# Walking the moving tiles and the outputs of five matmul stages in another order, with padded weight slots

## The chip, the cores and the metric

One core of one Trainium2 chip runs the whole program. The metric is the device time in microseconds (us); lower is better. "Before" is the kernel as it stood, "after" is the kernel with the change.

## What is computed

The reference is two transformer-like blocks over 512 tokens of width 1024, in float32, with a memory of 256 tokens. What matters here is its list of dense products, because nearly all the time is spent in them:

```
first_block:   proj = rms_norm(x) @ w_in          (front)
               mixers: gated delta rule, sparse attention, convolution
               x += concat(mixers) @ w_out
               x += cross attention with the memory (w_q, w_kv, w_o)
               x += square(relu(rms_norm(x) @ mlp_w1)) @ mlp_w2      (up and dn, in two halves)
second_block:  proj = rmsnorm(x) @ w_in_2, gates, convolution, recurrent unit      (mix)
               merged = sig(..) * (y_a @ w_out_a) + sig(..) * (y_b @ w_out_b)      (merge)
               x += merged @ w_o_2                                                 (w_o)
               x += (silu(h @ w_gate) * (h @ w_up)) @ w_down                       (ffn and down)
               rmsnorm(x)
```

## The kernel before, in words

Activations are held transposed: a tile is 128 features (partitions) by T = 512 tokens (2,048 bytes of each partition). Each activation and each weight is split in two float32r parts, a rounded `hi` and the rest `lo`. A product of a 128x128 weight block with a tile is three matmuls in the one helper `products` (L621 to L628, the matmul itself is L627): hi weights with the hi tile, hi weights with the lo tile, lo weights with the hi tile. All three add to one PSUM bank of 512 columns (`acc0` to `acc7`, in the program `k.ps`). Each matmul has its own weight load of 128 columns (512 bytes of each partition).

The weights arrive in panels of up to 8 blocks (PANEL = 1024 columns, 4,096 bytes). SyncE starts a DMA of a panel to one of two `raw` buffers (L522), ScalarE rounds it to `w_hi` (L1384), VectorE subtracts to get `w_lo` (L1981); in the front GpSimd takes part (L553). `w_hi` and `w_lo` have SPLIT = 4 slots each, and the slots lie back to back (`Panels.slot`, L468 to L471). A slot is handed back by the last matmul of a panel (`s_panel_used`).

`tensor_program` sets the order of TensorE's work by hand; the other engines follow by semaphores. `panel` (L630 to L646) runs a panel's blocks over the tiles t of an activation. Where it matters here, the stages come in this order, with the number of matmuls of 512 columns that each has:

- front, w_out, cross attention: 3 x (192 + 64 + 32 + 32) = 960, among many small matmuls;
- up0 and up1: 16 panels x 8 tiles x 3 = 384 each (`h_hi`, `h_lo` move);
- dn0 and dn1: 8 outputs x 16 tiles x 3 = 384 each (`u_hi`, `u_lo` move);
- mix: 8 turns x 58 blocks x 3 = 1,392 (`h`, and two blocks of `ub` a turn);
- merge: 2 x 8 outputs x 8 tiles x 3 = 384 (`ya`, `yb`);
- w_o: 8 x 8 x 3 = 192 (`mg`);
- ffn: 44 panels x 8 x 3 = 1,056 (`h`);
- down: 8 outputs x 22 tiles x 3 = 528 (`f`).

VectorE reads each finished bank (L2384, L2523, L2546, L2628, L2651, L2670) and hands it back (`acc_free`).

`plan_memory` lays the buffers out by hand. The first of them, `raw`, begins at byte 1,152 of a partition; `w_lo` and `w_hi` follow it at distances that are multiples of 4,096 bytes, so every weight block begins 128 bytes past a multiple of 512. The line `top[0] += (192 - top[0]) % 512` puts `h_hi` 192 bytes past a multiple of 512, and all of `h`, `u`, `f`, `y`, `ya`, `yb` and `mg` follow at multiples of 2,048 bytes. So in every product of these the moving tile begins 64 bytes past the weight block, counted modulo 512. `ub_hi` and `ub_lo` lie in the buffer `sq` instead, 70,432 bytes after `raw`: they begin 288 bytes past the weight block, modulo 512.

Of the kernel before, what the change touches and what calls it, by code (L numbers as in the profile page):

```python
# [18 lines left out]
P = 128  # L19
# [6 lines left out]
EPS = 1e-6  # L26
BLK = 8
PANEL = BLK * P
RAW = 2
SPLIT = 4  # L30
LEAD = 10
# [136 lines left out]
def plan_memory(nc, ctx):  # L168
# [286 lines left out]
class Panels(Count):  # L455
# [159 lines left out]
def tensor_program(nc, k):  # L615
# [5 lines left out]
    blk = k.const[:, C_BLK:C_BLK + P]  # L621
    tri = k.const[:, C_TRI:C_TRI + P]

    def products(out, w_at, wn, a_hi, a_lo, first, last):
# [5 lines left out]
    def panel(out, hi, lo, tiles, first=True, last=True, at=0, done=True, w=T, ready=None):  # L630

        slot = pan.slot().start
        if at == 0:

            e.wait_ge(k.s_split_done, RAW + pan.at(1))
        for n, t in enumerate(tiles):
            if ready:
                e.wait_ge(ready[0], ready[1] + t + 1)  # L640
            mm = products(out, slot + (at + n) * P, P, hi[:, t * w:(t + 1) * w], lo[:, t * w:(t + 1) * w],
                          first and n == 0, last and n == len(tiles) - 1)
        if done:
            mm.then_inc(k.s_panel_used, 1)
            pan.step()
        return mm  # L646
# [419 lines left out]
    for j in range(0, KT, 2):  # L1066

        width = 2 if j == 0 else 1
        for j0 in range(j, j + 2, width):
            outs = [acc.take(e, 4 + (j0 + n) % 2) for n in range(width)]  # L1070
            slots = []
            for n in range(width):
                e.wait_ge(k.s_split_done, RAW + pan.at(1))
                slots.append(pan.slot().start)
                pan.step()
            for t in range(KT):
                if t < HEADS:
                    e.wait_ge(k.s_go_lo, t + 1)
                elif t >= 6:
                    e.wait_ge(k.s_mix_lo, t - 5)  # L1080
                else:
                    e.wait_ge(k.s_att_lo, TT)
                for out, slot in zip(outs, slots):
                    mm = products(out[:], slot + t * P, P, til(k.y_hi, t), til(k.y_lo, t), t == 0, t == KT - 1)
# [55 lines left out]
    def wo_part(tiles, heads):  # L1140

        for n in tiles:
            if heads[0] == 0:
                acc.take(e, n)
                if n % 2 == 0:
                    e.wait_ge(k.s_split_done, RAW + pan.at(1))
                    wo_slots.append(pan.slot().start)
                    pan.step()
            for h in heads:
                e.wait_ge(k.s_ao_lo_done, h + 1)  # L1150
                mm = products(k.ps[n][:], wo_slots[n // 2] + (HEADS * (n % 2) + h) * P, P, til(k.ao_hi, h), til(k.ao_lo, h),
                              h == 0, h == HEADS - 1)
            if h == HEADS - 1:
                mm.then_inc((k.s_wo_first, k.s_panel_used)[n % 2], 1)

# [47 lines left out]
    for a, b in ((0, 4), (4, 6), (6, 7), (7, KT)):  # L1203

        for n in range(2):
            if a == 0:
                acc.take(e, n)
                e.wait_ge(k.s_split_done, RAW + pan.at(1))
                up_slots.append(pan.slot().start)
                pan.step()  # L1210
            for t in range(a, b):
                e.wait_ge(k.s_fed_lo, 3 * KT + t + 1)
                mm = products(k.ps[n][:], up_slots[n] + t * P, P, til(k.h_hi, t), til(k.h_lo, t), t == 0, t == KT - 1)
            if b == KT:
                mm.then_inc(k.s_panel_used, 1)
                if n == 0:
                    sum_squares(4 * KT, 3, k.sqacc)
    for j in range(2, 4):
        panel(acc.take(e, j)[:], k.h_hi, k.h_lo, range(KT))
    for half in range(2):  # L1220

        with e.Fori(0, MTH // 4 - (half == 0)) as i:
            pan.enter(i, 4)
            acc.enter(i, [2, 2, 0, 0, 0, 0, 0, 0])
            for j in range(4):
                panel(acc.take(e, j % 2)[:], k.h_hi, k.h_lo, range(KT))
            pan.leave(MTH // 4 - (half == 0))
            acc.leave(MTH // 4 - (half == 0))
        with e.Fori(0, KT // 2) as i:
            pan.enter(i, 4)  # L1230
            acc.enter(i, [1, 1, 0, 0, 0, 0, 0, 0])
            for j in range(2):
                out = acc.take(e, j)[:]
                ready = (k.s_up_lo, MTH * half)
                panel(out, k.u_hi, k.u_lo, range(0, 8), last=False, ready=ready)
                panel(out, k.u_hi, k.u_lo, range(8, 16), first=False, ready=ready)
            pan.leave(KT // 2)
            acc.leave(KT // 2)

# [6 lines left out]
    def mix_tile(u_lo, opening):  # L1246

        for a, b in zip(MIX_CUTS, MIX_CUTS[1:]):
            e.wait_ge(k.s_split_done, RAW + pan.at(1))
            slot = pan.slot().start  # L1250
            order = list(range(a, b))
            if opening and a < KT <= b:

                order = [n for n in order if n != KT - 1] + [KT - 1]
            for n in order:
                bank, hi, lo, t, first, last = blocks[n]
                if hi is k.ub_hi:
# [4 lines left out]
                mm = products(out[:], slot + (n - a) * P, P, til(hi, t), til(lo, t), first, last)  # L1262
# [16 lines left out]
    for n, (hi, lo) in enumerate(both):  # L1279
        out = acc.take(e, n)  # L1280
        e.wait_ge(k.s_split_done, RAW + pan.at(1))
        slots.append(pan.slot().start)
        for t in range(KT - 1):
            e.wait_ge(k.s_s2_free, t + 1)
            products(out[:], slots[n] + t * P, P, til(hi, t), til(lo, t), t == 0, False)
        pan.step()
    e.wait_ge(k.s_s2_free, KT)
    for n, (hi, lo) in enumerate(both):
        t = KT - 1
        products(k.ps[n][:], slots[n] + t * P, P, til(hi, t), til(lo, t), False, True).then_inc(k.s_panel_used, 1)  # L1290
    for n, (hi, lo) in enumerate(both):
        panel(acc.take(e, 2 + n)[:], hi, lo, range(KT))
    with e.Fori(0, KT // 2 - 1) as i:
        pan.enter(i, 4)
        acc.enter(i, [1, 1, 1, 1, 0, 0, 0, 0])
        for j in range(2):
            for n, (hi, lo) in enumerate(both):
                panel(acc.take(e, 2 * j + n)[:], hi, lo, range(KT))
        pan.leave(KT // 2 - 1)
        acc.leave(KT // 2 - 1)  # L1300


    with e.Fori(0, 2) as i:
        pan.enter(i, 4)
        acc.enter(i, [2, 2, 0, 0, 0, 0, 0, 0])
        for j in range(4):
            panel(acc.take(e, j % 2)[:], k.mg_hi, k.mg_lo, range(KT), ready=(k.s_mg_lo, 0))
        pan.leave(2)
        acc.leave(2)


    for j in range(4):
        panel(acc.take(e, j)[:], k.h_hi, k.h_lo, range(KT), ready=(k.s_fed_lo, 5 * KT))
        if j == 0:
            sum_squares(6 * KT, 5, k.sqacc)
    with e.Fori(0, FFN // 2 - 1) as i:
        pan.enter(i, 4)
        acc.enter(i, [1, 1, 1, 1, 0, 0, 0, 0])
        for j in range(4):
            panel(acc.take(e, j)[:], k.h_hi, k.h_lo, range(KT))  # L1320
        pan.leave(FFN // 2 - 1)
        acc.leave(FFN // 2 - 1)
    with e.Fori(0, KT // 2) as i:
        pan.enter(i, 8)
        acc.enter(i, [1, 1, 0, 0, 0, 0, 0, 0])
        for j in range(2):
            out = acc.take(e, j)[:]
            for a, b in zip(DOWN_CUTS, DOWN_CUTS[1:]):
                panel(out, k.f_hi, k.f_lo, range(a, b), first=a == 0, last=b == FFN,
                      ready=(k.s_f_lo_done, 0))  # L1330
        pan.leave(KT // 2)
        acc.leave(KT // 2)

# [1472 lines left out]
```

## Time and profile before

| | us |
|---|---|
| median of 2 runs | 1629.03 (1627.74 to 1630.31) |
| span of the profiled execution | 1626.4 |
| its own time less its span | not listed; the median stands 2.6 above the span |
| mean granted TensorE clock | 0.997 of full speed |
| TensorE busy with matmuls | 1595.6 (98% of the span) |

A busy TensorE is not a TensorE at its peak: a matmul is booked from its first column to its last result, so neighbours overlap in the record (a 512-column matmul is booked with some 390 ns), and the distance from one start to the next is what counts. The program starts with loads and norms, the front lasts to about 445 us, the dense stages fill 445 to 1,614 us, and the last norm and the output end the span.

### The profile page before, as it was taken

The numbers are of one execution on the slowest core, as the hardware profiler recorded it, in microseconds if no ns is written. First come the engines' busy times: TensorE is split into PE (matmuls) and PEld (weight loads), VectorE is DVE, ScalarE is ACT, GpSimd is POOL, SyncE is SP. The second block draws the span as 40 slices with busy tenths as digits, with TensorE's granted clock in tenths as the row PEclk, the third lists the DMA queues.
The fourth block names the chain that finished last, engine by engine and source line by source line (L and its number), as shares of the span: only waits on it lengthen the run. The fifth ranks groups of instructions, "written<-read, shape, count | busy, mean of one in ns | idle before, by whom it ended". The sixth has DMA issues, their size and how long they took to land.

```text
span 1626.4 us, 21588 instructions
## 1 busy us (share of the span) xinstructions
PE 1595.6 (98%) x7524; PEld 1311.0 (81%) x7524; DVE 912.4 (56%) x1319; ACT 684.1 (42%) x996; POOL 157.1 (10%) x97
## 2 busy tenths in 40 slices
PE   6999999999999999999999999999999999999997
PEld 5888798788788888888888888888888888888886
DVE  4549799765664323444377666666455544444332
ACT  5735554554653213433244545554224434443221
POOL 3445486100000000000000000000000000000000
PEclk9999999999999999999999999999999999999999
DMA  7521100122123232233233333333322323222332
GB/s 286 165 78 65 52 1 2 65 86 96 40 91 103 91 103 90 90 104 103 59 105 106 93 93 93 93 93 104 104 90 91 104 90 102 91 93 86 99 97 77
DMA packets 45665, 149.50 MB, mean 92 GB/s; under 512 B 4784, under 2 KB 5936, under 8 KB 45616
## 3 DMA queue, kind: packets, MB, share of 16 engines
q1 hardware_dynamic: 42240, 139.90, 27.1%
q10 hardware_dynamic: 3376, 8.95, 1.5%
q8 instruction: 31, 0.51, 0.1%
q14 instruction: 18, 0.15, 0.0%
HBM read 146.47 MB, written 2.10 MB: 91 GB/s over the span
## 4 chain that ended last, share of the span: by engine, by line
PE 91%; DVE 6%; DMA 1%; ACT 1%; issue 0%; ACTq 0%; DVEq 0%; SPq 0%
PE acc L627 84%; DVE c_acc L2105 1%; DVE tok L2243 1%; DMA x<-xT 1%; DVE d_score_a L2246 1%; PE acc L938 1%; DVE d_score_b L2246 1%; PE acc L963 1%; PE acc L1113 0%; PE acc L1134 0%; DVE g_x L2229 0%; PE acc L800 0%; PE acc L702 0%; DVE w_lo L1973 0%; DVE x L2681 0%
## 5 line engine op out<-in xcount | busy, mean ns | idle before, releaser
L627 PE MATMUL acc<-h_hi,w_hi 128*128 128x512 f32 x1248 | 492.3, 394 | 1.4 <-issue 0.8
L627 PE MATMUL acc<-h_hi,w_lo 128*128 128x512 f32 x1248 | 491.6, 394 | 0.0
L627 PE MATMUL acc<-h_lo,w_hi 128*128 128x512 f32 x1248 | 488.7, 392 | 0.0
L1981 DVE TENSOR_TENSOR w_lo<-raw,w_hi 128x1024 fp32r<-128x1024 f32 (+2 forms) x241 | 281.5, 1171 | 81.7 <-ACT w_hi L1384 59.7
L1384 ACT ACTIVATE w_hi<-raw 128x1024 fp32r<-128x1024 f32 (+2 forms) x241 | 241.9, 1007 | 178.2 <-PE acc L627 86.4
L627 PEld LDWEIGHTS acc<-h_hi,w_hi 128*128 128x128 f32 x1248 | 234.8, 188 | 54.3 <-issue 3.8
L627 PEld LDWEIGHTS acc<-h_lo,w_hi 128*128 128x128 f32 x1248 | 234.9, 188 | 53.4 <-issue 1.0
L627 PEld LDWEIGHTS acc<-h_hi,w_lo 128*128 128x128 f32 x1248 | 234.9, 188 | 49.2
L627 PE MATMUL acc<-u_hi,w_hi 128*128 128x512 f32 x256 | 100.9, 394 | 0.0
L627 PE MATMUL acc<-u_hi,w_lo 128*128 128x512 f32 x256 | 100.4, 392 | 0.0
L2384 DVE TENSOR_TENSOR x<-x,acc 128x512 f32 x32 | 22.0, 688 | 139.2 <-PE acc L627 138.7
L627 PE MATMUL acc<-u_lo,w_hi 128*128 128x512 f32 x256 | 99.3, 388 | 0.0
L2651 DVE TENSOR_TENSOR f_t<-acc,rstd 128x512 f32<-128x512 f32 x44 | 30.4, 691 | 98.5 <-PE acc L627 98.3
L627 PE MATMUL acc<-f_hi,w_lo 128*128 128x512 f32 x176 | 69.3, 394 | 0.0
L627 PE MATMUL acc<-f_lo,w_hi 128*128 128x512 f32 x176 | 69.0, 392 | 0.0
L553 POOL TENSOR_TENSOR w_lo<-raw,w_hi 128x1024 fp32r<-128x1024 f32 x25 | 61.3, 2452 | 78.5 <-ACT w_hi L1377 78.2
L627 PE MATMUL acc<-f_hi,w_hi 128*128 128x512 f32 x176 | 68.3, 388 | 0.0
L1911 ACT ACTIVATE f_hi<-f_t 128x512 f32 x22 | 13.9, 632 | 116.5 <-DVE f_t L2657 116.5
L1825 ACT ACTIVATE u_t<-u_t 128x512 f32<-128x512 f32 x32 | 20.2, 632 | 93.9 <-DVEq L2526 88.8
L2523 DVE SCALAR_TENSOR_TENSOR u_t<-acc,rstd 128x512 f32<-128x512 f32 x28 | 19.4, 691 | 69.1 <-PE acc L627 69.1
L627 PEld LDWEIGHTS acc<-u_hi,w_lo 128*128 128x128 f32 x256 | 48.1, 188 | 11.3
L627 PEld LDWEIGHTS acc<-u_lo,w_hi 128*128 128x128 f32 x256 | 48.1, 188 | 10.8
(394 smaller groups left out, 2323.1 us busy)
## 6 DMA issues: line engine op xcount, KB each, us to landing
raw<-panels_a SPq DMA_DIRECT2D x112, 512.0 KB, 3.3
raw<-panels_b SPq DMA_DIRECT2D x68, 512.0 KB, 3.3
raw<-mix SPq DMA_DIRECT2D x48, 448.0 KB, 3.4
raw<-mix SPq DMA_DIRECT2D x16, 512.0 KB, 3.7
raw<-down SPq DMA_DIRECT2D x16, 384.0 KB, 3.2
raw<-down SPq DMA_DIRECT2D x16, 320.0 KB, 2.9
x<-xT ACTq DMA_DIRECT2D x4, 1024.0 KB, 9.5
x_rows<-xN ACTq DMA_DIRECT2D x2, 1024.0 KB, 8.6
```

The costliest lines, as they stand in the source:

```text
L553: TTn(lo, raw, hi.bitcast(F32), ALU.subtract).then_inc(k.s_split_done, 1)
L627: mm = e.matmul(out, w[:, w_at:w_at + wn], a, start=first and n == 0, stop=last and n == 2)
L938: e.matmul(k.ps[4 + u % 2][:, 0:(qt + 1) * P], k.d_q[r, (h // 2) * T + qt * P:(h // 2) * T + (qt + 1) * P], k.d_k[r, 0:(qt + 1) * P], star ...
L963: mm = e.matmul(k.ps[(7, 3)[qt % 2]][:, h * 64:(h + 1) * 64], k.d_pt[:, (u % 2) * T + t * P:(u % 2) * T + (t + 1) * P], k.d_v[:, t * 64:(t ...
L1384: A(k.w_hi[:, ahead.slot(w)], k.raw[:, ahead.unsplit(w)], ACT.Copy).then_inc(k.s_weights_hi, 1)
L1825: A(k.u_t[:, (2 + j % 2) * T:(3 + j % 2) * T], k.u_t[:, (j % 2) * T:(j % 2 + 1) * T], ACT.Square).then_inc(k.s_up_sq, 1)
L1981: TTn(lo, raw, k.w_hi[:, ahead.slot(w)].bitcast(F32), ALU.subtract).then_inc(k.s_split_done, 1)
L2105: ins = STT(out=out, in0=y, scalar=w, in1=out, op0=ALU.mult, op1=ALU.add)
L2246: replaced[qt] = link(e.match_replace(scores[qt], tok(TOK_M8 + 8 * qt - 8, 8), scores[qt], TAKEN))
L2384: TTn(x, x, k.ps[b][:], ALU.add).then_inc(k.acc_free[b], 1)
L2523: STT(out=til(k.u_t, j % 2), in0=k.ps[j % 2][:], scalar=0.0, in1=k.rstd[:], op0=ALU.max, op1=ALU.mult).then_inc(k.acc_free[j % 2], 1)
L2651: TTn(til(k.f_t, j + 2 * n), k.ps[b][:], k.rstd[:], ALU.mult).then_inc(k.acc_free[b], 1)
```

## The change

Nothing is computed otherwise: the same three matmuls per block, with the same operands. What is new is the order in which a matmul goes over the 512 columns of its moving tile, with the same order over its output, and the place of the weight slots.

- `walked(ap, (side, run, back))` views 512 columns as `side` parts, each cut into pieces of `run` columns. It goes over the pieces of all parts side by side: piece c of part 0, piece c of part 1, and so on, then piece c + 1; with `back` it begins with the last c. Inside a piece it goes forward. With side 2 the two parts lie 1,024 bytes apart; with side 4 they lie 512 bytes apart. A piece of 4, 8, 16 or 32 columns is 16, 32, 64 or 128 bytes.
- The table ORDER has one entry for each stage: none for front, mix and w_o; (2, 16, back) for up0; (2, 4, back) for dn0; (2, 16, forward) for up1; (1, 16, back) for dn1; (2, 32, back) for merge; (4, 16, back) for ffn; (2, 8, back) for down.
- A slot of `w_hi` and `w_lo` is 64 bytes longer than a panel. `w_hi` begins 256 bytes later, all that follows it 512 bytes later (so `h` stays at 192 modulo 512).

```diff
+SLOT = PANEL + 16
+ORDER = {"front": None, "up0": (2, 16, True), "dn0": (2, 4, True), "up1": (2, 16, False), "dn1": (1, 16, True), "mix": None, "merge": (2, 32, True), "w_o": None, "ffn": (4, 16, True), "down": (2, 8, True)}
...
-    k.w_lo, _ = sb("w_lo", SPLIT * PANEL, F32R)
-    k.w_hi, _ = sb("w_hi", SPLIT * PANEL, F32R)
+    k.w_lo, _ = sb("w_lo", SPLIT * SLOT, F32R)
+    k.w_hi, _ = sb("w_hi", SPLIT * SLOT, F32R)
...
-        at = (self.base + self.n) % SPLIT * PANEL
+        at = (self.base + self.n) % SPLIT * SLOT
...
+def walked(ap, order):
+
+    if order is None or ap.shape[-1] != T:
+        return ap
+    side, run, back = order
+    v = ap.rearrange("p (s c r) -> p c s r", s=side, r=run)
+    return v[:, ::-1] if back else v
...
-            mm = e.matmul(out, w[:, w_at:w_at + wn], a, start=first and n == 0, stop=last and n == 2)
+            at = slot + block * P
+            mm = e.matmul(walked(out, order), w[:, at:at + P], walked(a, order), start=first and n == 0, stop=last and n == 2)
```

The rest of the diff hands the stage's entry of ORDER down to `products`; `blocks`, a new parameter of it, is not used.

## Rows read from the trace of the kernel before

**Rows 1.** The page: span, busy time and share of each engine.

```profile
span 1626.4 us, 21588 instructions
...
PE 1595.6 (98%) x7524; PEld 1311.0 (81%) x7524; DVE 912.4 (56%) x1319; ACT 684.1 (42%) x996; POOL 157.1 (10%) x97
...
PEclk9999999999999999999999999999999999999999
```

**Rows 2.** Chain of waits from 430 us to the end, by line.

```profile
by line: PE acc L627 98.3%; DVE x L2681 0.4%; DVE rstd L1964 0.3%; PE acc L654 0.2%; ACT L1920 0.1%; PE acc L1345 0.1%; DVE w_lo L1981 0.1%; ACT rstd L1390 0.1%; DVE x L2670 0.1%; DVEq L2685 0.1%; ACT sq L1368 0.1%; issue 0.0%; PE acc L1134
```

**Rows 3.** Windows by stage: length, busy PE, PEld, DVE, ACT, POOL; clock, DMA.

```profile
534.02:621.68 87.66, 87.66 (x384) 71.93 (x383) 25.67 (x26) 18.14 (x18) 0.00 (x0) 1.00 0.30 96
621.91:709.58 87.67, 87.67 (x385) 71.94 (x384) 41.04 (x47) 34.29 (x46) 0.00 (x0) 1.00 0.29 96
709.80:797.47 87.67, 87.67 (x385) 71.93 (x383) 35.13 (x40) 26.07 (x32) 0.00 (x0) 1.00 0.29 93
797.70:1118.16 320.46, 319.81 (x1395) 261.52 (x1393) 219.62 (x277) 159.49 (x194) 0.00 (x0) 1.00 0.33 94
1118.39:1206.05 87.66, 87.66 (x384) 71.93 (x383) 43.74 (x53) 21.28 (x24) 0.00 (x0) 1.00 0.31 102
1206.28:1249.99 43.71, 43.71 (x192) 35.87 (x191) 25.94 (x33) 16.98 (x23) 0.00 (x0) 1.00 0.29 96
1250.22:1492.57 242.35, 242.35 (x1059) 198.52 (x1057) 116.02 (x133) 100.58 (x112) 0.00 (x0) 1.00 0.28 93
1492.80:1613.65 120.85, 120.85 (x529) 99.16 (x528) 39.15 (x48) 27.10 (x37) 0.00 (x0) 1.00 0.30 84
```

**Rows 4.** Matmuls that read f_hi: count, durations in ns, first and last start.

```profile
L627 PE MATMUL acc<-f_hi,w_hi x176: 388/388/389, 1492.8 to 1613.0; 128*128 128x512 f32 x176
```

**Rows 5.** Timeline of TensorE around the two ub blocks (start, us).

```profile
900.97 0.39 PE L627 MATMUL acc<-h_hi,w_lo 128*128 128x512 f32 x1
901.20 0.40 PE L627 MATMUL acc<-ub_hi,w_hi 128*128 128x512 f32 x1
...
902.60 0.40 PE L627 MATMUL acc<-h_hi,w_hi 128*128 128x512 f32 x1
```

**Rows 6.** Timeline: float32 matmuls of 512 columns, merged.

```profile
165.85 3.17 PE L800 MATMUL acc<-proj,small_w 128*128 128x512 f32 x7
```

**Rows 7.** Timeline: float32 matmuls of 256 columns, merged.

```profile
411.01 1.89 PE L1113 MATMUL acc<-xk,a_q 128*128 128x256 f32 x8
```

**Rows 8.** Groups by form: mean ns of one such matmul.

```profile
L1113 PE MATMUL acc<-xk,a_q 128*128 128x256 f32 x32 | 7.9, 387 | 0.2 <-ACT a_p L1773 0.2
...
L800 PE MATMUL acc<-proj,small_w 128*128 128x512 f32 x16 | 7.0, 592 | 0.0
```

**Rows 9.** Timeline of TensorE, float32r matmuls of 256 columns.

```profile
22.73 0.28 PE L627 MATMUL acc<-m_hi,w_hi 128*128 128x256 f32 x1
...
24.96 0.28 PE L627 MATMUL acc<-m_lo,w_hi 128*128 128x256 f32 x1
```

**Rows 10.** Waits: who waited for whom, us in total, times, longest.

```profile
ACT w_hi L1384 <- PE acc L627: 86.4, 29, 4.3
...
ACT w_hi L1384 <- DMA raw<-panels_a: 50.3, 15, 6.0
```

**Rows 11.** The page: VectorE's and ScalarE's split of a panel; DMA to landing.

```profile
L1981 DVE TENSOR_TENSOR w_lo<-raw,w_hi 128x1024 fp32r<-128x1024 f32 (+2 forms) x241 | 281.5, 1171 | 81.7 <-ACT w_hi L1384 59.7
L1384 ACT ACTIVATE w_hi<-raw 128x1024 fp32r<-128x1024 f32 (+2 forms) x241 | 241.9, 1007 | 178.2 <-PE acc L627 86.4
...
raw<-panels_b SPq DMA_DIRECT2D x68, 512.0 KB, 3.3
```

**Rows 12.** Timeline of the end.

```profile
1613.42 0.39 PE L627 MATMUL acc<-f_hi,w_lo 128*128 128x512 f32 x1
...
1618.38 5.36 DVE L2681 SCALAR_TENSOR_TENSOR x<-x,vec,acc 128x512 f32<-128x512 f32 x8 [1.33 <-PE acc L1345]
```

More of the change, by code:

```diff
@@ L622, in tensor_program, with products, panel @@
     tri = k.const[:, C_TRI:C_TRI + P]
-    def products(out, w_at, wn, a_hi, a_lo, first, last):
+    def products(out, slot, block, a_hi, a_lo, first, last, order, blocks=KT):
         for n, (w, a) in enumerate(((k.w_hi, a_hi), (k.w_hi, a_lo), (k.w_lo, a_hi))):
-            mm = e.matmul(out, w[:, w_at:w_at + wn], a, start=first and n == 0, stop=last and n == 2)
+            at = slot + block * P
+            mm = e.matmul(walked(out, order), w[:, at:at + P], walked(a, order), start=first and n == 0, stop=last and n == 2)
         return mm
-    def panel(out, hi, lo, tiles, first=True, last=True, at=0, done=True, w=T, ready=None):
+    def panel(out, hi, lo, tiles, first=True, last=True, at=0, done=True, w=T, ready=None, order=ORDER["front"], blocks=KT):
         slot = pan.slot().start
@@ L640, in panel @@
                 e.wait_ge(ready[0], ready[1] + t + 1)
-            mm = products(out, slot + (at + n) * P, P, hi[:, t * w:(t + 1) * w], lo[:, t * w:(t + 1) * w],
-                          first and n == 0, last and n == len(tiles) - 1)
+            mm = products(out, slot, at + n, hi[:, t * w:(t + 1) * w], lo[:, t * w:(t + 1) * w],
+                          first and n == 0, last and n == len(tiles) - 1, order, blocks)
         if done:
@@ L1218, in tensor_program @@
     for j in range(2, 4):
-        panel(acc.take(e, j)[:], k.h_hi, k.h_lo, range(KT))
+        panel(acc.take(e, j)[:], k.h_hi, k.h_lo, range(KT), order=ORDER["up0"])
     for half in range(2):
@@ L1225, in tensor_program @@
             for j in range(4):
-                panel(acc.take(e, j % 2)[:], k.h_hi, k.h_lo, range(KT))
+                panel(acc.take(e, j % 2)[:], k.h_hi, k.h_lo, range(KT), order=ORDER[f"up{half}"])
             pan.leave(MTH // 4 - (half == 0))
@@ L1234, in tensor_program @@
                 ready = (k.s_up_lo, MTH * half)
-                panel(out, k.u_hi, k.u_lo, range(0, 8), last=False, ready=ready)
-                panel(out, k.u_hi, k.u_lo, range(8, 16), first=False, ready=ready)
+                panel(out, k.u_hi, k.u_lo, range(0, 8), last=False, ready=ready, order=ORDER[f"dn{half}"])
+                panel(out, k.u_hi, k.u_lo, range(8, 16), first=False, ready=ready, order=ORDER[f"dn{half}"])
             pan.leave(KT // 2)
@@ L1261, in mix_tile @@
                 out = acc.take(e, bank) if first else k.ps[bank]
-                mm = products(out[:], slot + (n - a) * P, P, til(hi, t), til(lo, t), first, last)
+                mm = products(out[:], slot, n - a, til(hi, t), til(lo, t), first, last, ORDER["mix"], b - a)
             mm.then_inc(k.s_panel_used, 1)
@@ L1289, in tensor_program @@
         t = KT - 1
-        products(k.ps[n][:], slots[n] + t * P, P, til(hi, t), til(lo, t), False, True).then_inc(k.s_panel_used, 1)
+        products(k.ps[n][:], slots[n], t, til(hi, t), til(lo, t), False, True, ORDER["merge"]).then_inc(k.s_panel_used, 1)
     for n, (hi, lo) in enumerate(both):
-        panel(acc.take(e, 2 + n)[:], hi, lo, range(KT))
+        panel(acc.take(e, 2 + n)[:], hi, lo, range(KT), order=ORDER["merge"])
     with e.Fori(0, KT // 2 - 1) as i:
@@ L1297, in tensor_program @@
             for n, (hi, lo) in enumerate(both):
-                panel(acc.take(e, 2 * j + n)[:], hi, lo, range(KT))
+                panel(acc.take(e, 2 * j + n)[:], hi, lo, range(KT), order=ORDER["merge"])
         pan.leave(KT // 2 - 1)
@@ L1306, in tensor_program @@
         for j in range(4):
-            panel(acc.take(e, j % 2)[:], k.mg_hi, k.mg_lo, range(KT), ready=(k.s_mg_lo, 0))
+            panel(acc.take(e, j % 2)[:], k.mg_hi, k.mg_lo, range(KT), ready=(k.s_mg_lo, 0), order=ORDER["w_o"])
         pan.leave(2)
@@ L1312, in tensor_program @@
     for j in range(4):
-        panel(acc.take(e, j)[:], k.h_hi, k.h_lo, range(KT), ready=(k.s_fed_lo, 5 * KT))
+        panel(acc.take(e, j)[:], k.h_hi, k.h_lo, range(KT), ready=(k.s_fed_lo, 5 * KT), order=ORDER["ffn"])
         if j == 0:
@@ L1319, in tensor_program @@
         for j in range(4):
-            panel(acc.take(e, j)[:], k.h_hi, k.h_lo, range(KT))
+            panel(acc.take(e, j)[:], k.h_hi, k.h_lo, range(KT), order=ORDER["ffn"])
         pan.leave(FFN // 2 - 1)
@@ L1329, in tensor_program @@
                 panel(out, k.f_hi, k.f_lo, range(a, b), first=a == 0, last=b == FFN,
-                      ready=(k.s_f_lo_done, 0))
+                      ready=(k.s_f_lo_done, 0), order=ORDER["down"], blocks=b - a)
         pan.leave(KT // 2)
```

10 lines of the change are left out of this document (5 added, 5 removed).

## The prediction, made before the run

> **What bounds the kernel now.** I read the page first: TensorE is busy 98% of a span of 1626.4 us and its granted clock is full in all 40 slices [rows 1]. The chain of waits says whether that matters: from 430 us to the end 98.3% of it is L627, the dense matmuls [rows 2]. The windows by stage show the same without gaps, at a granted clock of 1.00, with VectorE between 0.29 and 0.69 of each stage [rows 3]. So the time of the dense part is the number of matmuls times the distance from one start to the next, and nothing else. In down the matmuls that read `f_hi` with `w_hi` begin at 1492.8 and at 1613.0 us, 176 of them, each followed by two others: 120.2 us / (175 x 3) = 228.9 ns [rows 4]. The other stages agree: 87.66 us for 384 matmuls, 120.85 for 528, less the edges [rows 3].
>
> Is 228.9 ns what 512 columns must cost? The trace has three things beside it.
>
> The float32 matmuls, which are not split in hi and lo. Seven of 512 columns take 3.17 us as a block; less the 592 ns booked for the last, six distances are 2.578 us, 429.7 ns each [rows 6, 8]. Eight of 256 columns take 1.89 us; less 387 ns, seven distances of 214.7 ns [rows 7, 8]. Time goes with the columns and is twice what a column at 2.4 GHz takes (0.417 ns), so a pass over 512 columns costs half of 429.7, that is 214.8 ns, weight loads included. The float32r matmul goes over its columns at twice that speed and lies 14.1 ns above such a pass.
>
> The float32r matmuls of 256 columns: from 22.73 to 24.96 us lie 19 distances of 117.4 ns [rows 9], 10.0 ns above half of 214.7. So the excess is neither fixed per instruction nor quite proportional to the columns.
>
> The `ub` blocks: six matmuls from 901.20 to 902.60 us, 233.3 ns each [rows 5], in the middle of `h` matmuls at 228.9. Weights, clock and form are the same. What differs is where the moving tile begins against the weight block: 288 instead of 64 bytes past it, modulo 512. So the distance depends on addresses in SBUF, by 4.4 ns here. My reading, which no row proves: the moving stream and the load of the next 128 columns of weights, which runs beside every matmul (PEld busy 0.82 of each stage [rows 3]), get in each other's way when TensorE reads at full speed, and how often depends on how the two walk over addresses.
>
> The Trainium skill speaks against this reading. Its page "TensorE: Matmul & The Clock Gate", section "Step-by-step: what each phase is for", says that TensorE reads its moving operand and its weights through two independent SBUF ports, so that loading the next weights takes nothing from the running matmul. By that rule the excess would come from something else and the new order would gain nothing; the address dependence of the `ub` blocks doesn't agree with it, and the rule stands behind my first rival.
>
> **The change, part by part.** It adds no instruction, no wait and no transfer: 7,524 matmuls stay 7,524. It touches 384 x 4 (up0, dn0, up1, dn1) + 384 (merge) + 1,056 (ffn) + 528 (down) = 3,504 matmuls by their order, and the other 2,544 of 512 columns (960 in the front part, 1,392 in mix, 192 in w_o) only by the place of the weight slots.
>
> *The order.* The trace of before has no walked matmul, so I bound it from both sides. Best: the whole excess goes, 14.1 ns x 3,504 = 49 us. Worst: the address generator loses a column's time at each jump. The jumps of one matmul are 512 / run: 32 in up0, up1, dn1 and ffn, 128 in dn0, 16 in merge, 64 in down. In all 384 x (32 + 32 + 32 + 128 + 16) + 1,056 x 32 + 528 x 64 = 159,744 jumps; at 0.417 ns, 67 us lost. A milder bad case is that the walked stages go the way of `ub`: 4.4 x 3,504 = 15 us lost. What picks a value between them is the shape of the walk. A weight load passes over 512 bytes while the matmul passes over 2,048; with two parts side by side the moving stream advances through the addresses of one kilobyte at half its speed, with four parts at a quarter, which is the weight load's own pace (512 bytes in the time of a matmul). Two streams that go at like pace can stay clear of each other; two at unlike pace must meet again and again. That argument favours a gain, but it holds only if both go in the same direction and begin clear of each other, and up1 walks forward where up0 walks back, so at least one of these can't be the matching one. I take 8 ns of the 14.1, somewhat over half: 3,504 x 8 = 28 us less. By stage: up and dn 3.1 us each, merge 3.1, ffn 8.4, down 4.2.
>
> *The slots.* The moving tile now begins 64, 0, 448 and 384 bytes past `w_lo` in slots 0 to 3, modulo 512, and 320, 256, 192 and 128 bytes past `w_hi`, in place of 64 everywhere. In the unwalked stages that can cost as much as it costs `ub` (4.4 ns x 2,544 = 11 us) or gain the like. 64 lies among the new values once, and `ub`'s 288 lies between two of them. I take zero, with both ends in the range. For VectorE, ScalarE and the DMA 64 bytes more between slots change no length.
>
> *Does a faster TensorE get its weights?* A panel of 24 matmuls lasts 24 x 228.9 = 5.49 us and would last 5.30. Its supply is 3.3 us from issue to landing, 1.0 us on ScalarE, 1.2 us on VectorE, with two raw buffers [rows 11]. ScalarE waits for TensorE to free a slot (86.4 us, 29 times), more than for the panels' DMA [rows 10]; both mean that weights are ahead. VectorE has more than half of each walked stage's time to itself [rows 3]. So the gain stays. In mix, where VectorE has 219.6 of 320.5 us, nothing gets faster. The tail after the last matmul of down (1613.42 us to the end of the span, 13.0 us) is VectorE, ScalarE and output and stays [rows 12].
>
> The sum: 1626.4 - 28 + 0 = 1598.4 us of span. The median of the runs stands 2.6 us above the profiled span, so 1601 us.
>
> **The rivals.**
>
> *The order has nothing to do with it.* The excess belongs to float32r at full speed, say to each 128-column load, whatever the order. For: it is the same in every stage with tiles at 64, whatever tile or slot is read. Against: `ub`. Time: 1629, with the slots' 11 us either way.
>
> *The walk frees the stream wholly.* All 14.1 ns go, or 10 and more: 1629 - 35 to 49, that is 1580 to 1594; with a gain in the unwalked stages too, down to 1570. For: the float32 matmuls show that 214.8 ns per 512 columns is to be had with loads beside them, and the walked pace can equal the load's. Against: the different entries for like stages, which can't all match.
>
> *Each jump costs.* Place: L627 in dn0 first, which has 128 jumps a matmul, then down and ffn. Price: at one column's time a jump, dn0 20 us (49,152 jumps), down 14, ffn 14, in all 67, so 1696 us without a gain and 1668 with the 28. From 28 us / 159,744 = 0.18 ns a jump the change is slower than before. For: the output jumps as well as the input, and PSUM has not been written so in any row. Against: no row shows a jump costing anything, and pieces of 4 columns or more leave neighbours together. The Trainium skill bears on this one, on its page "Advanced Engine Details and Errata", section "Memory Cachelines": SBUF lines are of 16 bytes and PSUM's of 8, and "Any non-contiguous AP significantly slows down matmuls"; its next line softens this to two consecutive elements being enough. By the first sentence dn0 would be much slower, by the second nothing would; no run here shows either yet.
>
> **How the numbers follow.** The forecast, a gain of 3 to 10 ns on the walked matmuls (1594 to 1619 us with the slots at zero), gets 0.45. Nothing: 0.2. The whole excess: 0.22. Slower: 0.13, of which 0.08 over 2%. What a measurement of this kernel can tell from no change is about 2%, 33 us. Faster by over 2% means under 1596.4: the 0.22 and a third of the forecast's share with help from the slots, 0.38 in all. Slower by over 2% 0.08, the rest, 0.54, within. The range is 1577 to 1636: the whole excess in all walked stages less a little, to no gain with the slots' loss.
>
> **What would show it.** Right: matmuls that read `f_hi` about 221 ns apart and down some 116.6 us long, ffn some 234, dn0 and dn1 each 84.6; mix (320.5) and w_o (43.7) as before; as many instructions. The jump rival shows in dn0 alone first: its window grows from 87.7 to 108. The slots show in mix and w_o, which walk as before: a change there is theirs. If the stages differ among each other by more than 5 ns a matmul, the order's fit and not the walk as such decides. Wrong altogether: a lower granted clock, or stretches in which TensorE waits for `w_lo`.

## The result: slower by 2.7%, and the profile after

The median of the changed kernel is 1673.76 us (1673.48 to 1674.03) against 1629.03 (1627.74 to 1630.31): ratio 1.0274, 95% interval 1.0256 to 1.0292. Slower by 45 us, where I had forecast 28 us less, with a range that ended at 1636. Experiments whose time is given without a ratio were run once; their distances are read from the trace of that run.

The page of the changed kernel, its head:

```profile
span 1671.7 us, 21588 instructions
...
PE 1640.4 (98%) x7524; PEld 1316.4 (79%) x7524; DVE 914.8 (55%) x1319; ACT 684.1 (41%) x996; POOL 157.2 (9%) x97
...
PEclk9999999999999999999999999999999999999999
```

The instructions are as many as before, the granted clock is as high [rows 1], and the chain of waits from 430 us on is the dense matmuls again (the helper's line is L639 now):

```profile
by line: PE acc L639 98.2%; DVE x L2693 0.4%; DVE rstd L1976 0.3%; PE acc L666 0.2%; PE acc L1146 0.1%; ACT L1932 0.1%; PE acc L1357 0.1%; DVE w_lo L1993 0.1%; ACT rstd L1402 0.1%; DVE x L2682 0.1%; DVEq L2697 0.1%; ACT sq L1380 0.1%; issue
```

So no new wait took the time; the matmuls stand further apart. The windows by stage, changed kernel, each from the first matmul of a stage to the first of the next (stretch, length, busy PE, PEld, DVE, ACT, POOL, clock, DMA share, GB/s), in the order up0, dn0, up1, dn1, mix, merge, w_o, ffn, down:

```profile
447.70:537.27 89.57, 89.57 (x388) 72.40 (x386) 50.47 (x58) 40.91 (x55) 0.00 (x0) 1.00 0.29 99
537.27:635.09 97.82, 97.82 (x385) 72.77 (x384) 25.67 (x26) 18.21 (x18) 0.00 (x0) 1.00 0.27 86
635.09:727.25 92.16, 92.16 (x385) 72.81 (x384) 41.06 (x47) 34.29 (x46) 0.00 (x0) 1.00 0.26 91
727.25:817.57 90.32, 90.32 (x385) 72.16 (x384) 35.15 (x40) 26.04 (x32) 0.00 (x0) 1.00 0.28 90
817.57:1140.40 322.83, 322.26 (x1395) 261.93 (x1394) 220.12 (x277) 159.54 (x194) 0.00 (x0) 1.00 0.32 94
1140.40:1231.28 90.88, 90.88 (x385) 72.40 (x384) 43.65 (x53) 21.25 (x24) 0.00 (x0) 1.00 0.29 99
1231.28:1275.54 44.26, 44.26 (x194) 36.10 (x193) 25.95 (x33) 16.96 (x23) 0.00 (x0) 1.00 0.28 95
1275.54:1527.19 251.65, 251.65 (x1060) 200.93 (x1059) 116.07 (x133) 100.45 (x112) 0.00 (x0) 1.00 0.27 89
1527.19:1658.95 131.76, 131.76 (x529) 100.34 (x528) 39.17 (x48) 27.11 (x37) 0.00 (x0) 1.00 0.28 77
```

[Rows 3] end at a stage's last start, one distance of 0.23 us earlier, but for down; counted alike, dn0 grew by 9.9 us, down by 10.9, ffn 9.1, up1 4.3, merge 3.0, dn1 2.4, up0 0.8, and the stages that walk as before grew too: mix 2.1, w_o 0.3. With 2.4 in the front that is the 45.3 us between the spans. Length by count gives the distance from one start to the next: dn0 97.82 us / 384 = 254.7 ns, down 131.76 / 528 = 249.5, against 228.9. The distances below are taken in this way, or as the mean of the distances within a stage where a stage has a wait.

The waits fit weights that were ahead all the time: ScalarE waits for TensorE to free a slot for 150.0 us, 44 times, not for 86.4 [rows 10].

A distance given for a stage is a mean over its matmuls. In the kernel before, the successive distances in dn0 are 232, 226 and 229 ns over and over, with a nanosecond or so between repeats; their mean is the 228.9.

### The profile page after: what moved, and what is told of

Same layout as the page of the kernel before. It is cut to its first block, busy times and chain, and to the rows that moved or that the text cites. A ratio compares the mean times of both kernels' runs of the same rounds, so it can differ in the third digit from the quotient of the medians.

```text
span 1671.7 us, 21588 instructions
## 1 busy us (share of the span) xinstructions
PE 1640.4 (98%) x7524; PEld 1316.4 (79%) x7524; DVE 914.8 (55%) x1319; ACT 684.1 (41%) x996; POOL 157.2 (9%) x97
## 4 chain that ended last, share of the span: by engine, by line
PE 91%; DVE 5%; DMA 2%; ACT 1%; issue 0%; ACTq 0%; DVEq 0%; SPq 0%
PE acc L639 84%; DVE c_acc L2117 1%; DVE tok L2255 1%; DMA x<-xT 1%; DVE d_score_a L2258 1%; PE acc L950 1%; DVE d_score_b L2258 1%; PE acc L975 0%; DMA raw<-panels_a 0%; PE acc L1125 0%; PE acc L1146 0%; DVE g_x L2241 0%; DVE w_lo L1985 0%; PE acc L812 0%; PE acc L714 0%
## 5 line engine op out<-in xcount | busy, mean ns | idle before, releaser
L639 PE MATMUL acc<-h_hi,w_hi 128*128 128x512 f32 x1248 | 499.3, 400 | 1.3 <-issue 0.8
L639 PE MATMUL acc<-h_hi,w_lo 128*128 128x512 f32 x1248 | 495.2, 397 | 0.0
L639 PE MATMUL acc<-h_lo,w_hi 128*128 128x512 f32 x1248 | 495.0, 397 | 0.0
L639 PEld LDWEIGHTS acc<-h_hi,w_hi 128*128 128x128 f32 x1248 | 236.0, 189 | 59.6 <-issue 3.8
L639 PEld LDWEIGHTS acc<-h_hi,w_lo 128*128 128x128 f32 x1248 | 235.8, 189 | 55.9
L639 PEld LDWEIGHTS acc<-h_lo,w_hi 128*128 128x128 f32 x1248 | 235.8, 189 | 55.6 <-issue 1.0
L639 PE MATMUL acc<-u_lo,w_hi 128*128 128x512 f32 x256 | 104.8, 409 | 0.0
L639 PE MATMUL acc<-u_hi,w_lo 128*128 128x512 f32 x256 | 104.6, 408 | 0.0
L639 PE MATMUL acc<-u_hi,w_hi 128*128 128x512 f32 x256 | 104.5, 408 | 0.0
L639 PE MATMUL acc<-f_hi,w_hi 128*128 128x512 f32 x176 | 73.1, 415 | 0.0
L639 PE MATMUL acc<-f_hi,w_lo 128*128 128x512 f32 x176 | 73.0, 415 | 0.0
L639 PE MATMUL acc<-f_lo,w_hi 128*128 128x512 f32 x176 | 72.9, 414 | 0.0
L639 PEld LDWEIGHTS acc<-u_hi,w_lo 128*128 128x128 f32 x256 | 48.5, 189 | 14.4
L639 PEld LDWEIGHTS acc<-u_lo,w_hi 128*128 128x128 f32 x256 | 48.3, 189 | 14.4
```

The source lines that it names most:

```text
L639: mm = e.matmul(walked(out, order), w[:, at:at + P], walked(a, order), start=first and n == 0, stop=last and n == 2)
```

## Experiments

### The two halves of the change

`pad_only` has an ORDER of nothing but None; `walk_only` has the slots back to back:

```diff
-SLOT = PANEL + 16
+SLOT = PANEL
```

> The slots padded, nothing walked. The stages that the change leaves unwalked (mix, w_o) became 1.5 to 1.6 ns a matmul slower in the changed kernel. Theory 'the slots alone do that': every dense stage goes from 228.9 to about 230.4 ns, 6,048 matmuls x 1.5 ns = 9 us, so about 1638 us. Theory 'the walked stages around them do it': 1629 us, and mix stays at 228.9.

Measured: 1639.59 us, ratio 1.0059 (1.0042 to 1.0076). Every dense stage stands at 230.5 to 230.7 ns; mix and w_o:

```profile
802.49:1125.35 322.86, 322.29 (x1396) 261.94 (x1395) 220.09 (x277) 159.55 (x194) 0.00 (x0) 1.00 0.32 94
1213.88:1258.18 44.30, 44.30 (x193) 36.09 (x192) 25.95 (x33) 16.95 (x23) 0.00 (x0) 1.00 0.28 95
```

These are the changed kernel's lengths to 0.04 us. The slots alone cost 9 us. Sorted by slot, the matmuls of dn0 show four mean levels: 229.6, 227.1, 233.2 and 232.3 ns for slots 0 to 3, where before all were 228.9. The moving tile lies 64, 0, 192 and 128 bytes past the weight block there, modulo 256; modulo 512 the blocks of `w_hi` and `w_lo` lie 256 bytes apart. In slot 0 the tile begins 64 bytes past `w_lo` and 320 past `w_hi`, and the three products still have the distances of before, 231.7, 225.7 and 229.3 ns (231.6, 225.7 and 229.3): a shift by 256 bytes changed nothing.

> The order of the change on slots that lie back to back again. Theory 'walk and slots add up': dn0 some 253, down some 248, ffn 236.5, up1 238.5 ns a matmul, mix and w_o back at 228.9; in all 45 - 9 = 36 us over before, 1665. Theory 'the walk clashes with the padded slots, each was fitted to the other's absence': the walked stages come down to 229 or below, 1625 or less. If the pads help the walk (the matmul finds its place against the load), the walked stages get slower than in the changed kernel, over 1674.

Measured: 1672.77 us, ratio 1.026 (1.0243 to 1.0277). Mix is back at 229.1 and w_o at 229.0; the walked stages stand at up0 228.3, dn0 251.1, up1 240.0, dn1 237.8, merge 236.7, ffn 236.0, down 260.0. dn0 and down:

```profile
534.85:631.27 96.42, 96.42 (x386) 73.15 (x384) 25.67 (x26) 18.11 (x18) 0.00 (x0) 1.00 0.27 87
...
1520.34:1657.59 137.25, 137.25 (x529) 100.32 (x528) 39.16 (x48) 27.09 (x37) 0.00 (x0) 1.00 0.26 74
```

Neither theory as I put it: the halves don't add up (43 + 9 is over 45), since the pads bring down from 260.0 to 249.6 and dn1 from 237.8 to 235.2, and cost ffn, dn0 and up0 1.5 to 3.7 ns. The walk is most of the loss.

### Which side pays: the read or the write

```diff
# moving_only
-            mm = e.matmul(walked(out, order), w[:, at:at + P], walked(a, order), ...
+            mm = e.matmul(out, w[:, at:at + P], walked(a, order), ...
# output_only
+            mm = e.matmul(walked(out, order), w[:, at:at + P], a, ...
```

> Padded slots; only the moving tile is walked, the output goes in order, so each product's columns land permuted (the result is another one). Theory 'read side' (moving stream against weight load): the stages keep the distances of the changed kernel, dn0 254.8, down 249.6, up1 240.0, merge 236.7, total about 1674. Theory 'write side' (jumps in PSUM): all fall back to about 230.4 ns, total about 1638.

> Padded slots; only the output is walked, the moving tile goes in order (columns land permuted, the result is another one). Theory 'read side': about 230.4 ns in every stage, about 1638 us. Theory 'write side': dn0 254.8, down 249.6 ns and about 1674 us. If both sides cost, the two halves' excesses add up to that of the changed kernel.

Measured: 1675.65 and 1638.97 us (both leave the columns of a product out of order). dn0 and down, with only the moving tile walked:

```profile
538.44:636.26 97.82, 97.82 (x385) 72.77 (x384) 25.66 (x26) 18.21 (x18) 0.00 (x0) 1.00 0.27 86
1528.40:1660.16 131.76, 131.76 (x529) 100.35 (x528) 39.15 (x48) 27.12 (x37) 0.00 (x0) 1.00 0.27 77
```

and with only the output walked:

```profile
537.19:625.73 88.54, 88.54 (x386) 72.19 (x385) 25.67 (x26) 18.13 (x18) 0.00 (x0) 1.00 0.30 95
1502.72:1624.43 121.71, 121.71 (x530) 99.25 (x529) 39.17 (x48) 27.11 (x37) 0.00 (x0) 1.00 0.30 83
```

The first pair repeats the changed kernel to the hundredth, the second the kernel with the pads alone. All of the walk's price is on the read of the moving tile; jumping in PSUM costs nothing in the seven orders of the change, whose pieces are of 16 bytes and more (dn0 and down above). That disagrees with the Trainium skill's "Any non-contiguous AP significantly slows down matmuls" (page "Advanced Engine Details and Errata", section "Memory Cachelines"). Its next line, by which every two consecutive elements should be contiguous, is not contradicted: all these pieces hold at least four, and no run walked the output alone in shorter ones.

### Does the weight load take part?

`short_loads` loads fewer columns of weights in some stages; in `fixed_plain` and `fixed_walk` every load keeps its 128 columns, but reads the same one:

```diff
# short_loads, with m = 64 (dn0, up1, down) or 32 (dn1)
+                mm = e.matmul(walked(out[0:m], order), w[:, at:at + m], walked(a, order), ...
# fixed_plain, fixed_walk
+            mm = e.matmul(walked(out, order), w[:, at:at + 1].broadcast_to([P, P]) if a.shape[-1] == T else w[:, at:at + P], walked(a, order), ...
```

> Slots back to back. dn0 loads 64 columns of weights a matmul and dn1 32, in the plain order; up1 (walked 2,16 forward), down (2,8 back) load 64; ffn (4,16 back) keeps 128 as control; the output rows of the columns left out aren't computed. The moving reads stay as they were. Theory 'the weight load meets the moving stream': the excess over 214.8 ns falls with the load, dn0 from 14.1 to about 7 (222 ns), dn1 to about 3.5 (218), up1 from 25 to about 12.6 (227), down from 45 to about 23 (237). Theory 'the moving stream alone, it trips over its own jumps': dn0 and dn1 228.9, up1 240.0, down 260.0, ffn 236.0 as in the run with the walk alone.

Measured (1651.63 us; dn0 and dn1 walk plainly here): dn0 228.3, up1 240.0, dn1 231.7, down 245.3, ffn 236.0. Halving the load left the plain order (within 0.6 ns) and up1 where they were, quartering it made dn1 slower, and only down fell, by 14.7 of its 45 ns. The load is not a thing whose length is paid for. (A load of 64 or 32 columns also takes another form of the array, 128x64 and 128x32 in the records, so this run alone would not decide.)

> Slots back to back, plain order; each 128-column weight load of the 512-column products reads one column 128 times over, and so stays in one place of SBUF in place of passing over 512 bytes (all outputs of a product become equal: another result). The moving reads stay. Theory 'where the load reads decides whether it meets the moving stream': the 14.1 ns over the float32 pass change, to about 216 ns if a load that stands still meets it hardly ever. Theory 'a load costs its 128 columns wherever it reads' or 'the moving stream alone': 228.9 ns in every stage.

> The same fixed loads, with the order of the change, slots back to back. Moving stream alone: every stage as with the walk alone, up0 228.3, dn0 251.1, up1 240.0, dn1 237.8, merge 236.7, ffn 236.0, down 260.0. Loads against the stream: all of them move; up1 and merge, which didn't answer to the offset of the slots nor (up1) to a load of half the columns, are the ones that should stay if any do.

Measured (1645.40 and 1663.86 us): plain 231.7 ns in every stage but mix (231.5), where the load that moves on had 228.9; walked, up0 231.0, merge 233.4, dn1 233.3, ffn 235.0, down 240.0, but dn0 251.1 and up1 240.0 as before. dn0, up1 and down of `fixed_walk`:

```profile
537.43:633.85 96.42, 96.42 (x386) 73.15 (x385) 25.67 (x26) 18.12 (x18) 0.00 (x0) 1.00 0.27 87
633.85:726.01 92.16, 92.16 (x385) 72.20 (x384) 41.06 (x47) 34.31 (x46) 0.00 (x0) 1.00 0.27 91
1522.63:1649.34 126.71, 126.71 (x529) 99.79 (x528) 39.16 (x48) 27.09 (x37) 0.00 (x0) 1.00 0.28 80
```

So there are two parts. Where the load reads from matters in most stages (down: 20 ns of its excess, 260.0 to 240.0), and the plain order changed too, though a load itself is booked with 189 ns, against 188 where it reads its 128 columns. That disagrees with the rule of the Trainium skill's page "TensorE: Matmul & The Clock Gate", section "Step-by-step: what each phase is for", that the prediction weighed, by which a load takes nothing from the running matmul. up1 is the other part: 240.0 ns in all six runs that walk it as the change does, with padded slots and without, with half a load, with the load on one column, and at offset 0. There the price is the moving stream's own. dn0 has 251.08 ns with either load too, but it isn't free of the load: with the pads its slots stand at 254.3, 252.6, 256.5 and 255.6 ns.

### A grid of orders

A stage is a cell; each kernel changes the table ORDER alone. All at offset 64 with slots back to back, `grid_d` at offset 0.

> Slots back to back, another order in each stage, as cells of a grid: up0 (1,4,back), dn0 (1,8,back), up1 (1,64,back), dn1 (1,128,back), mix (1,32,back), merge (2,8,forward), w_o (4,16,forward), ffn (2,64,back), down (2,16,back). Known at the same offset: plain 228.9, (1,16,back) 237.8, (2,16,back) 228.3, (2,16,forward) 240.0, (2,32,back) 236.7, (4,16,back) 236.0, (2,8,back) 260.0, (2,4,back) 251.1. Theory 'a jump has a price': the excess falls with the length of the piece, (1,128) near 229 and (1,4) over 245. Theory 'it is the way the two streams meet': no such order by length; down with (2,16,back) must repeat 228.3, else the cells of different stages can't be compared.

> Slots back to back; orders that were seen in one stage are put into another: up0 (2,8,back), 260.0 in down; dn0, w_o and ffn (2,16,back), 228.3 in up0 and 233.3 in down; up1 (2,4,back), 251.1 in dn0; down (1,8,back), 233.3 in dn0; new are dn1 (4,4,back) and merge (4,8,back). If order and offset alone set the distance: the same figures again. If the panels' cut matters (down has 6, 6, 5, 5 blocks a panel, so its tiles and blocks stand otherwise to each other by 512 bytes): up0 differs from 260.0, and dn0, w_o and ffn agree with up0's 228.3. If pieces 1,024 bytes apart are the costly thing and not short pieces: all pairs with 4 or 8 columns stay over 250, down stays at 233, and (4,4) and (4,8) cost as much as the pairs.

> Slots back to back, offset 64; the distance between the parts is varied with short pieces: up0 (8,4,back) 256 bytes apart, dn0 (16,4,back) 128, up1 (8,8,back), dn1 (4,4,forward), merge (32,4,back) 64, w_o (4,64,back), ffn (8,16,back), down (4,4,back). Known: (1,4) 233.3, (2,4) 251.1, (4,4) 271.0, (2,8) 245.3 and 260.0, (4,8) 233.3. Theory 'reads that alternate between places far apart clash': the excess of pieces of 4 falls from (4,4) over (8,4) and (16,4) to (32,4), which with parts of 64 bytes is near to the plain order. Theory 'only the number of jumps counts': all three with pieces of 4 have 128 jumps and cost alike; already against it is (1,4) at 233.3. Direction: (4,4,forward) against 271.0 back.

Measured: 1647.16, 1662.77 and 1711.32 us. Distances in ns, with plain at 228.9; parts of 512 / side columns:

| pieces of | 1 part | 1,024 B apart | 512 B | 256 B | 128 B | 64 B |
|---|---|---|---|---|---|---|
| 16 bytes, back | 233.3 | 251.1 | 271.0 | 277.8 | 240.2 | 220.0 |
| 32 bytes, back | 233.3 | 245.3 / 260.0 | 233.3 | 266.8 | 237.0 | 233.3 |
| 64 bytes, back | 237.8 | 228.3 / 233.3 | 236.0 | 237.8 | 237.9 | |
| 128 bytes, back | 233.4 | 236.7 | | | | |
| 256 bytes, back | 228.9 | 229.0 | 228.9 | | | |

(The cells of 32 bytes at 128 B and 64 B, and of 64 bytes at 128 B, come from `grid_e` below.) Forward: (2,8) 243.3, (2,16) 240.0, (4,16) 236.5, (4,4) 269.3. The worst and the best window of `grid_c`, up0 (8,4,back) and merge (32,4,back):

```profile
445.90:553.52 107.62, 107.62 (x387) 74.46 (x386) 50.77 (x58) 42.75 (x55) 0.00 (x0) 1.00 0.24 82
...
1172.30:1256.79 84.49, 84.49 (x386) 71.92 (x384) 43.75 (x53) 21.26 (x24) 0.00 (x0) 1.00 0.31 106
```

Each of the six orders in the first row has 128 pieces a matmul, and they lie between 220 and 278 ns: a jump has no price of its own. All that differs between these six is how far apart the places are between which the reads alternate. The distance doesn't simply fall with the step, as the first theory of `grid_c` had it: 256 bytes apart is worse than 512. Pieces of 256 bytes cost nothing with up to four parts. Two things did not come out as I expected. (2,16,back) had 228.3 to 228.4 in four stages and 233.3 in down, and (2,8,back) 245.3 in up0 and 260.0 in down: order and offset modulo 512 alone don't set the distance. The cut that `grid_b` suspected (down's panels hold 6, 6, 5 and 5 blocks) is not the reason: in the first panel of each output tile and block go in step as in the other stages, and its matmuls stand at 260.0 and 233.3 ns like the rest of down. What the plan of memory leaves is that `f_lo` lies 45,056 bytes behind `f_hi`, where the other walked tiles have 16,384 or 32,768; no run tests that. (1,8), (2,4) and (4,4), each seen in two stages, did repeat. So most cells are one stage's figure, and a cell may be off by 5 to 15 ns elsewhere. And the distance is not a smooth function of anything in the table.

### The better offset

> Order of the change, slots back to back, activations 128 and not 192 bytes past a multiple of 512, so that moving tiles begin where the weight blocks do (modulo 512). In the run with padded slots alone the slot at this offset had 227.1 ns, the ones at 64, 128 and 192 (modulo 256) 229.5, 232.3 and 233. Theory 'offset and order act together': each stage moves, dn0 by the run with both changes 251 to 253, up0 to about 233, dn1 to about 233.5. Theory 'offset and order are separate': every stage 1.8 ns below the run with the walk alone.

> The kernel before with activations 128 bytes past a multiple of 512: no walk, no pad, moving tile and weight block begin together modulo 512. If the offset sets the distance: 227.1 ns a matmul in every dense stage, 6,048 x 1.8 ns = 11 us less, about 1618 us. If slot 1's 227.1 came from its neighbours in the padded run: no change, 1629 us.

```diff
-    top[0] += (192 - top[0]) % 512
+    top[0] += (128 - top[0]) % 512
```

`plain_at0`: 1618.55 us, ratio 0.9939 (0.9923 to 0.9956); 226.7 to 226.8 ns in every dense stage but mix, whose `ub` blocks keep their place (227.1). In down:

```profile
1480.79:1600.47 119.68, 119.68 (x529) 99.10 (x528) 39.16 (x48) 27.09 (x37) 0.00 (x0) 1.00 0.30 84
```

Nearly all single distances of down are 226 or 227 ns now, where they were 225 to 232. The offset moves the distance in the plain order. `walk_at0`: 1668.14 us; up0 230.4, dn0 253.3, up1 240.0, dn1 233.3, merge 236.7, ffn 239.9, down 251.7. Offset and order act together, up1 and merge excepted, which don't answer to the offset at all.

> Plain order, activations 128 past a multiple of 512, slots padded by 16 bytes: moving tile less weight block is 0, 240, 224, 208 (w_lo) and 192, 176, 160, 144 (w_hi) in slots 0 to 3, modulo 256. Known: 226.7 at 0, 228.9 at 64, about 233 at 192, 232.3 at 128, 233.3 at 32 (ub). If the offset counts in steps of 64 bytes only, all slots lie between 229 and 233 by a mixture of the two loads; if finer, some slot lies below 226.7 and a faster place exists.

Measured: mean distances by slot of 231.6, 229.7, 234.4 and 232.1 ns, and 1647.89 us. No better place among these; steps of 16 bytes matter.

> Slots back to back, activations at 128 modulo 512 (offset 0, plain 226.7): up0 (1,64,back), dn0 (2,64,back), up1 (1,4,back), dn1 (4,8,back), mix (2,16,back), merge (4,16,forward), w_o (1,32,back), ffn (1,128,back), down (4,64,back). Known at offset 64: (1,64), (1,128), (2,64) equal the plain order there; (1,4), (4,8) and (1,32) 233.3. Theory 'long pieces leave the plain distance': (1,64), (1,128), (2,64) and (4,64) at 226.7. If walking back can win at all, some stage lies below 226.7 and a walked kernel would beat both; if none does, the plain order at offset 0 is the best that these runs know. mix with (2,16,back) should repeat up0's 230.4 of the run with the walk at offset 0.

Measured (1632.36 us): (1,64), (2,64), (1,128) and (4,64) at 226.7 to 226.8, (1,4) 233.3, (4,8) 232.3, (4,16,forward) 231.2, (1,32) 232.4, mix with (2,16,back) 233.2 and not up0's 230.4. Long pieces keep the plain distance; none of these orders lies below it.

### A walk that beats both kernels

```diff
-ORDER = {"front": None, "up0": (2, 16, True), ...
+ORDER = {"front": (32, 4, True), "up0": (32, 4, True), ...
```

> Slots back to back, offset 64, every product of 512 columns (front, mix and w_o too) walked as (32,4,back): 32 parts 64 bytes apart, pieces of 16 bytes. In merge that had 220.0 ns against 228.9 plain. Theory 'this walk meets the loads less, wherever it is used': 6,048 x 8.9 ns = 54 us less, 1576 us, unless weights or VectorE in mix become late. Theory 'it was merge's own' (two activations in turn, loads in that rhythm): merge alone at 220, the rest at 229 or above, 1625 or more.

Measured: 1581.37 us (1579.59 to 1583.03), ratio 0.970 (0.9684 to 0.9717) against the kernel before. The same walk gives 220.0 to 220.1 ns in up, dn, merge, ffn and down, 221.1 in mix, 226.0 in w_o. dn0 and down:

```profile
527.83:612.31 84.48, 84.48 (x386) 71.91 (x384) 25.66 (x26) 18.13 (x18) 0.00 (x0) 1.00 0.31 100
...
1452.35:1568.52 116.17, 116.17 (x529) 98.88 (x528) 39.15 (x48) 27.13 (x37) 0.00 (x0) 1.00 0.31 87
```

The gain belongs to the walk and not to merge. 48 of the 54 us came: w_o gave 2.8 ns a matmul and not 8.9, and the front, with small matmuls and waits between, became 2.8 us shorter where 960 matmuls would have given 8.5. Why w_o gives less, with a tile that begins 64 bytes past the weight block as elsewhere, is open. Weights were not late, since ScalarE still waited for slots:

```profile
ACT w_hi L1396 <- PE acc L639: 76.9, 27, 3.9
```

> Neighbours of that walk: up0 (64,4,back) 32 bytes apart, dn0 (32,4,forward), up1 (32,8,back), dn1 (16,8,back), mix (32,4,back), merge (128,2,back), w_o (16,16,back), ffn (64,2,back), down (32,2,back). Theory 'each read goes to another place of a bank pattern of 64 bytes, and steps of 64 bytes keep the moving stream off the load': the walks with 32 parts of 64 bytes stay near 220 forward and back, and others don't. If the stream alone gets faster by short steps between parts: (64,4) below 220. Pieces of 8 bytes (the three with run 2) cost more if the rule on 16-byte lines holds: two reads per line in place of one.

Measured (2064.84 us): dn0 (32,4,forward) 223.3, up0 (64,4,back) 233.1, up1 (32,8,back) 233.3, dn1 (16,8,back) 237.0, w_o (16,16,back) 237.9, mix (32,4,back) 221.1. With pieces of 8 bytes: merge (128,2) 453.3, ffn (64,2) 461.1, down (32,2) 433.3. The window of merge:

```profile
1113.08:1287.14 174.06, 174.06 (x385) 79.75 (x384) 44.27 (x53) 21.19 (x24) 0.00 (x0) 1.00 0.15 51
```

Among the orders tried, only the 16-byte piece with the 64-byte step gains; its direction is worth 3 ns. Pieces of 8 bytes, in the moving tile and in the output at once, take nearly twice the time. The Trainium skill's page "SBUF — State Buffer", section "Specifications (TRN2)", gives SBUF lines of 16 bytes, asks for at least two hits on a line for full bandwidth, and names a penalty for each cross to a new line. Pieces of 8 bytes cross twice as often as whole lines, in whatever order those come. The first agrees with the trace if the crossings are what counts (433 to 461 ns); if two float32 elements of a line are already its two hits, it does not. The rule has nothing that tells the orders of whole lines apart, and they lie between 220 and 278 ns.

> The order (32,4,back) in every stage, slots back to back, activations at 128 modulo 512. In the plain order the offset 0 gave 2.2 ns a matmul over offset 64. If walk and offset add up: 217.8 ns and 13 us below the 1581 of the same walk at offset 64. If the walk takes the offset's place (a stream that steps 64 bytes at a time has no one offset to the load): 220 again, 1581 us. If they clash as the change's orders did: above 220.

Measured: 1616.16 us, ratio 0.992 (0.9904 to 0.9937), 226.6 to 226.8 ns in the dense stages from dn0 on but w_o, which has 222.8. The offset that helps the plain order costs this walk 6.7 of its 8.9 ns a matmul, and helps it in w_o alone.

> The order (32,4,back) everywhere, slots padded by 16 bytes, activations at 192: moving tile less weight block 64, 48, 32, 16 (w_lo) and 0, 240, 224, 208 (w_hi) modulo 256 in slots 0 to 3. In the plain order 16-byte steps gave 229 to 236 ns a slot. If the walk is indifferent to the offset: 220 in all slots, 1581 us. If it is not: the slots differ by several ns, and the best of them names a better place.

Measured: 1613.51 us; in dn0 the slots stand at 229.1, 224.5, 227.7 and 222.2 ns. This walk is not indifferent to the offset either.

## Why the prediction was wrong, step by step

- **What bounds the kernel**: right. The time is the number of dense matmuls times their distance; the 45 us are in the distances, with the chain at 98.2% L639 and no new wait.
- **The distance depends on addresses in SBUF**, read from the `ub` blocks: right, and worth more than the 4.4 ns seen there. The offset alone moved the plain order from 226.7 to 233.2 ns. That the weight load takes part was right for most stages (down 260.0 to 240.0 with a load that stands still), and wrong for up1, which keeps 240.0 ns whatever the load does.
- **The order, "I take 8 ns of the 14.1"**: this is the step that failed. "Two streams that go at like pace can stay clear of each other" has no support: ffn, walked at what I called the load's own pace, lost 7 to 8.6 ns, dn0 22 to 26, down 21 to 31; only up0 gained anything without pads (0.5 ns). In place of -28 us the walked stages cost 40 us, pads included. The argument looked only at the meeting with the load. With the moving tile alone walked, the price is there in full (dn0 254.8 ns, down 249.6); with the output alone walked, none of it. In up1 it doesn't depend on the load at all, and no row of before could show such a price. The bounds of this term (49 us less, 67 more) held the result. I chose between them by an argument that no row bore out, gave 0.08 to slower by over 2%, and cut the range at its upper end.
- **The slots, "I take zero"**: mis-sized, but inside its bounds. The term was for the 2,544 unwalked matmuls, and they cost 4.8 us (front 2.4, mix 2.1, w_o 0.3) of the 11 at its bad end; with nothing walked, the pads cost 9 us over all 6,048 (1.0059). Two of four slots went to offsets that cost 3.4 and 4.3 ns, one gained 1.8. The row of `ub` had said that an offset off 64 can cost; it was one row against none for a gain.
- **From the span to the time**: the sum added 2.6 us. In the runs the time lies 1.8 or 1.9 us above the span of the same execution, which changes nothing here.
- **Supply**: right. ScalarE waited for slots before and after, and at 220 ns too.
- **The rival "the order has nothing to do with it"**: wrong. `walk_only` is slower by 2.6% with nothing but the order changed.
- **The rival "each jump costs"**: right in sign, and dn0 did grow more per matmul than any other in the changed kernel, but to 97.8 us and not 108, and down grows more in `walk_only`. That its 1668 us with the forecast's gain lies near the 1674 measured is luck. As a mechanism it fell: 128 jumps cost 4.4 ns in one part and gain 8.9 in parts of 64 bytes.
- **The rival "frees the stream wholly"**: wrong for this change. But 220.0 ns shows that nine of the fourteen ns were there to be had, by another walk.

Still open is the pattern behind the table: why 512 and 256 bytes apart are worst and 64 best, and why down and w_o differ from other stages under the same order. The plain order has the same distances at 64 and at 320 bytes; I leave that period unexplained too. How the price splits between reading and writing for pieces of 8 bytes wasn't tried.

## What to carry to other kernels

Where TensorE's matmuls bound a kernel, compare the distance from start to start with another form's in the same trace; an excess of a few ns a matmul can be the order and the place of the reads, and both are free to change. Don't reason out a good order: put a different one in each stage of one kernel, read the distances, and spread the best; here the third such kernel had the cell that was worth three per cent, and the neighbours of that cell lose. Try the best cell in every stage before you count on it, since w_o and down didn't always follow the others. Pads and offsets must be chosen together with the order, since the best offset of one order took the gain of another away.

## What the runs showed of the hardware that I had not expected

- A float32r matmul of 512 columns takes from 220.0 to 277.8 ns by the order in which it reads whole 16-byte pieces of its tile, at one granted clock; the order of its writes to PSUM didn't matter in the seven orders tried (dn0 230.5 ns with or without).
- With pieces of 8 bytes in the moving tile and the output it takes 433 to 461 ns.
- The offset of the moving tile against the weight block is worth 226.7 ns (0) to 233.2 ns (192, modulo 256) in the plain order; slots padded by 16 bytes gave means from 229.7 to 234.4.
- The walked order of up1, two parts of 64-byte pieces forward, takes 240.0 ns at any offset and with any load tried.
- A weight load that reads one column 128 times is not lighter on the stream: the plain order went from 228.9 to 231.7 ns.
